# Samples' attention: a 512-column product of a constant ahead of each group of four transposes

## The reference, cut to what matters

```python
D_MODEL, HEAD_DIM, KV_HEADS, HEADS_PER_GROUP = 1024, 64, 2, 4     # 8 heads
# q: (8 samples, 1, 2, 4, 64); ks_blk, vs_blk: 2048 past rows + the new one, in blocks of 64
_, idx = lax.top_k(score, min(N_SEL_BLOCKS, nsel))     # score: from the compressed branch
k_sel, v_sel = ks_blk[bi, gi, idx], vs_blk[bi, gi, idx]
s_s = jnp.einsum('bqghd,bgqkld->bghqkl', q, k_sel) * scale + b_s
o_s = jnp.einsum('bghqm,bgqmd->bqghd', masked_softmax(s_s, tpos <= qp), v_sel)
s_w = jnp.einsum('bqghd,bkgd->bghqk', q, kw) * scale + rel_bias_heads(rel_bias, dw)
o_w = jnp.einsum('bghqk,bkgd->bqghd', masked_softmax(s_w, window_mask), vw)
o = g[..., 0:1] * o_c + g[..., 1:2] * o_s + g[..., 2:3] * o_w
```

## Time and profile before

| | |
|---|---|
| median of 3 runs | 2104.97 us |
| lowest, highest | 2093.45, 2114.90 us |
| profiled execution: time | 2103.55 us |
| its span | 2101.7 us |
| TensorE (PE) busy in the span | 1978.6 us, 94% |
| PE weight loads | 1899.4 us, 90% |
| VectorE (DVE), ScalarE (ACT), GpSimd (POOL) busy | 830.1, 647.1, 795.4 us |
| mean granted TensorE clock | 0.961 |

### The profile page before, as it was taken

One profiled execution on the slowest core, in us unless ns is written; L12 is line 12 of the kernel. 1 busy time (PEld: TensorE's weight loads), 2 busy tenths in 40 slices (PEclk: granted clock), 3 DMA queues, 4 the chain that ended last, 5 costly groups with the idle time before them and its releaser, 6 DMA issues. The chain is left out here.

```text
span 2101.7 us, 35304 instructions
## 1 busy us (share of the span) xinstructions
PE 1978.6 (94%) x14462; PEld 1899.4 (90%) x14462; DVE 830.1 (39%) x1560; ACT 647.1 (31%) x1159; POOL 795.4 (38%) x639
## 2 busy tenths in 40 slices
PE   7999989966799998999989899999999999999899
PEld 6999989944678888999989899999999999999699
DVE  4013534323677875112241359333333430322633
ACT  5112035422577674001011223223332310200333
POOL 2223300000345454333333215777777733332140
PEclk9999989977899999999999889999999999999999
DMA  7233374343400002111113121222332232321212
GB/s 245 62 91 121 81 244 161 121 162 129 149 2 2 1 2 82 46 46 46 46 36 131 41 108 49 76 90 81 120 101 80 80 121 74 119 79 51 81 41 81
DMA packets 168156, 182.62 MB, mean 87 GB/s; under 512 B 21176, under 2 KB 151810, under 8 KB 165154
## 3 DMA queue, kind: packets, MB, share of 16 engines
q1 hardware_dynamic: 162034, 131.48, 20.1%
q0 software_dynamic: 2304, 33.56, 4.1%
q10 hardware_dynamic: 3696, 15.86, 2.0%
HBM read 148.12 MB, written 36.94 MB: 88 GB/s over the span
## 5 line engine op out<-in xcount | busy, mean ns | idle before, releaser
L603 POOL CAST WS<-W 128x1024 fp32r<-128x1024 f32 (+1 forms) x87 | 96.3, 1106 | 551.2 <-PE proj_acc L595 147.6
L2480 PE MATMUL ffn_acc<-ZR,WR 128*128 128x258 f32 x1976 | 293.9, 283 | 0.6 <-POOL WR L2405 0.6
L2480 PEld LDWEIGHTS ffn_acc<-ZR,WR 128*128 128x128 f32 x1976 | 262.0, 190 | 0.8 <-POOL WR L2405 0.8
L605 POOL TENSOR_TENSOR WS<-W,WS 128x1024 fp32r<-128x1024 f32 (+1 forms) x87 | 215.0, 2471 | 7.0
L2405 POOL TENSOR_TENSOR WR<-WQ,WR 128x512 fp32r<-128x512 f32 x114 | 172.0, 1515 | 101.4 <-ACT WR L2618 101.4
L2480 PE MATMUL ffn_acc<-HH,WR 128*128 128x258 f32 x1216 | 202.3, 283 | 3.5 <-issue 2.2
L2733 DVE TENSOR_TENSOR E<-E,ffn_acc 128x516 f32<-128x516 f32 x133 | 92.0, 692 | 237.6 <-PE ffn_acc L2480 234.8
L595 PE MATMUL proj_acc<-HH,WS 128*128 128x344 f32 x912 | 174.3, 324 | 7.6 <-DVE HL L527 7.6
L2480 PEld LDWEIGHTS ffn_acc<-HH,WR 128*128 128x128 f32 x1216 | 170.1, 190 | 4.0 <-issue 2.5
L595 PEld LDWEIGHTS proj_acc<-HH,WS 128*128 128x128 f32 x912 | 149.0, 189 | 8.4 <-issue 6.1
L595 PE MATMUL merge_acc<-HH,WS 128*128 128x344 f32 x768 | 146.9, 324 | 6.8 <-DVE HL L527 6.8
(11 more groups left out here) (480 smaller groups left out, 4152.5 us busy)
## 6 DMA issues: line engine op xcount, KB each, us to landing
W<-in_w_in SPq DMA_DIRECT2D x30, 512.0 KB, 3.9
gated_values<-E ACTq DMA_DIRECT2D x22, 516.0 KB
WQ<-in_w_ffn_up SPq DMA_DIRECT2D x38, 256.0 KB, 2.9
WQ<-in_w_ffn_gate SPq DMA_DIRECT2D x38, 256.0 KB, 3.1
W<-in_w_ffn_down SPq DMA_DIRECT2D x16, 384.0 KB, 3.1
W<-in_w_ffn_down SPq DMA_DIRECT2D x16, 320.0 KB, 3.0
kept_x<-Z SPq DMA_DIRECT2D x1, 4128.0 KB, 13.3
Z<-kept_x SPq DMA_DIRECT2D x1, 4128.0 KB, 13.4
```

What stands on the lines that cost most here:

```text
L603: k.nc.gpsimd.tensor_copy(k.WS[:, ws, 0, 0:nk, :], w).then_inc(hi_done, 1)
L605: k.nc.gpsimd.tensor_tensor(k.WS[:, ws, 1, 0:nk, :], w, k.WS[:, ws, 0, 0:nk, :].bitcast(F32), ALU.subtract).then_inc(split_done, 1)
L2480: last = nc.tensor.matmul(acc[:, b + h, 0:QN], k.WR[:, RING[j], part, c, :], src[:, c, h * QN:(h + 1) * QN], start=(c == 0 and part == 0 a ...
```

## The change

Each group of four transposes, in `keys` and in `turn_p`, gets one product ahead of it: 128x128 weights and 512 columns, both taken from `QZ` as float32r, written to the whole bank that the four transposes overwrite. It stands behind the wait for the bank. There are 50: 40 in `keys`, 10 in `turn_p`. `QZ` is filled once, at the head of VectorE's list, with eight copies of the 128x128 identity, and TensorE waits for that (`dense_in`) ahead of its first product of the stage.

```diff
+        (dense_in,) = st.sems("dense_in")
+        dense = k.QZ[:].rearrange("p a b c m -> p (a b c m)")
...
                 bank = tp_bank(pe, ("keys", i, q, j))
+                nc.tensor.matmul(bank, dense[:, 0:P], dense[:, 512:1024], start=True, stop=True)
                 for x in range(4):
...
                 bank = tp_bank(pe, ("p", i, x, 0))
+                nc.tensor.matmul(bank, dense[:, 0:P], dense[:, 512:1024], start=True, stop=True)
                 src = (PA, PA, PB, PB, PW)[x][:, (0, 512, 0, 512, 0)[x]:]
...
+            pe.wait_ge(dense_in, 1)
             pe.wait_ge(k.sel_in, 7 * 16)
             pe.wait_ge(qs_placed, 4)
...
         def _(dve):
+            nc.vector.tensor_copy(dense.rearrange("p (r m) -> p r m", r=8), k.ident[:].unsqueeze(1).to_broadcast([P, 8, P])).then_inc(dense_in, 1)
             nc.vector.memset(QS, 0.0).then_inc(qs_placed, 1)
```

## The result

The changed kernel takes 2116.09 us (median of 20 runs, 2106.64 to 2123.33) against 2102.82 us for the kernel before, measured beside it (20 runs). The ratio is 1.0061, with a 95% interval of 1.005 to 1.0072: 13 us slower, within the 1% that was called "same", inside the range of 2098 to 2121, and 6 us above the number 2109.9. The profiled execution of the changed kernel has a span of 2119.4 us, before 2101.7: 17.7 us more. It took 2121.24 us and so is 5 us above the median of its kernel.

A forecast was written before the change was run, and what follows sets the result against it. PE's own work, partly at half clock, was taken to bound the samples' attention. Cast 1.1 plus products 13.5 less 1.0 absorbed is 13.6 us; less 7.25 for A held, 6.35 us slower: 2109.9 us, range 2098 to 2121.

The forecast's parts named there:

- A is held: Samples' attention, 447.2 to 460.9 us: the added products keep the clock at 1.00 there, giving back 7.25 us.
- A: Samples' attention from 447.2 us: 13.7 us at 0.50 of the clock, forecast to run at 1.00.
- Rival 1: Samples' attention: the clock stays where it was and the products only cost; 13.6 us slower, 2117.2 us; chance 0.33.
- B: Samples' attention from 474.5 us: 3.4 us at 0.50 of the clock, forecast to stay so.
- Between them it is at 1.00: Samples' attention: the clock was read as 1.00 between the four stretches at 0.50.
- C: Samples' attention from 502.7 us: 9.4 us at 0.50 of the clock, forecast to stay so.
- Cast, 1.1 us: Head of VectorE's list: the cast that fills QZ delays PE's first product of the stage by 1.1 us, nothing hiding it.
- Products, 0.23 and 0.43 us: Groups of transposes: each added product costs 0.23 us at clock 1.00 and 0.43 at 0.50; 44 on the path, 13.5 us.
- Rival 1's sum, 13.6 us: Samples' attention without any clock change: 1.1 for the cast, 13.5 for products, less 1.0 absorbed by bank copies.
- the clock in the stages behind moving: Stages after the samples' attention: example given for "something else", the case outside forecast and rivals; chance 0.03.
- The six hidden products: Half 1's groups of samples 4, 5 and 6: six products, 2.6 us, fit under PE's waits of 7.99 and 4.17 us.

The follow-up runs named there:

- keys-only kernel: The kernel before plus the cast and the forty products ahead of the keys' groups, none ahead of P's turns: 2111.23 us, ratio 1.0035.
- the change with the fill: The changed kernel plus twelve unread products in the feed-forward stage where PE waits for the rounded rows: 2107.58 us, ratio 1.004 to the kernel before.
- the kernel with the feed-forward fill alone: The kernel before plus twelve unread products in the feed-forward stage where PE waits for the rounded rows: 2100.96 us, ratio 1.0006.

## Why the prediction was right or wrong

The range held and the chances of "same" too, but only since the range was wide enough for the rival. The number was 6 us low, and the failed step is **"A is held"**. I gave back 7.25 us for it; the trace gives back nothing there. The argument for it compared the share of full-array products (0.23 in each 0.67 us of a group) with that of `scores` between 460.9 and 474.5, and took an equal share as enough. That was a likeness and no evidence: it compared a stretch that already had 1.00 with one that had to get there. The runs show in its place that the clock in A stays at 0.50 with one product per group. Three kernels with one product per group have A at 0.50 for 13.7 us or more, two kernels with two products have 3.4. Rival 1's chance of 0.33 was too small beside the 0.45 of the forecast. But rival 1 isn't the mechanism either. It said that the clock is where it was, and B, which the forecast left at 0.50, was at 1.00 in all five kernels with products ahead of the turns.

**A reading of the earlier trace rows.** "Between them it is at 1.00" is not so between B and C: the clock was at 0.50 from 491.6 on, mostly while PE waited for the gathers. The sum doesn't change by it, since the two groups in that time lie under a wait.

**Cast, 1.1 us.** It took 0.69, below even the lower bound of 0.91 for clearing the buffer. With the 0.07 us to the next start and the 0.24 by which the copy of `relb` is longer it cost 1.0, so the term was nearly right by a part that wasn't in it.

**Products, 0.23 and 0.43 us.** 0.38 at 0.50. At 1.00 a set of four groups grew by 0.79 us where 0.67 was worked out from the banks' rhythm: the copies absorb 0.13 of four products, not 0.25.

**Rival 1's sum, 13.6 us, to the stage.** The total came out at 13.3, but not as summed. To the end of half 0 the profile has +8.3 us where "about 8" stood, with A 6.8 us longer than before, which wasn't predicted. In the keys-only kernel and in the change with the fill, A was 13.7 us, and the time from the stage's first product to the gather was 49.5 and 49.1 us against 44.8 before: +4.7 and +4.3, not 7. Behind it, 19 products less the absorption should have added about 5.5 us more (8 x 0.43 + 11 x 0.23 - 0.5 for the copies), and +0.17 came; in the pair with the fill it is +3.9 (62.0 against 58.1). In the changed kernel's profile C ended 6.4 us sooner against sample 7's keys, worth up to 3.2, and sample 6's keys came 10.92 us after their gather's start and not 12.21, worth 1.3 (gathers at 492.64 and 484.37). Whether the product did the first is open, and the other runs speak against it: with the same products C ended 8.1 and 8.5 us after sample 7's keys (keys only; change with the fill), and 7.9 us in the kernel with the feed-forward fill alone, which has none. Nor is the second clearly the product's: sample 6's keys came 10.8 to 12.7 us after the gather in twelve profiles, 10.91 in the one with the cast only.

**The stage as a whole.** From its first product to the prompt's attention it is 110.7 and 111.1 us in the two profiles that hold the change, and 101.7 to 105.7 in six that hold nothing of it but, in one, the cast. So some 7 us is the change's, against 13.6 minus the cast predicted. With the cast that is about the 8.3 and 8.8 us of S x c in the two pairs, though these count another thing. The spread of the six has a part that can be seen: where the clock was at 1.00 for 3.4 us just ahead of A, half 0 took 44.8 us, and where that was missing, 47.1.

**The stages behind: 0.03 for "the clock in the stages behind moving".** That was the second miss, though it does not change the verdict. In the profile 9.6 us arise there. In the medians it is some 5 us, if the stage took 8 of the 13; that is argued. I had summed the stage to its last wait and taken the rest as a constant, while the page's slices 23 and 24 of the earlier trace rows show another dip to 0.8 that a shift of 8 us can lengthen or shorten.

**The gathers and waits.** 4.61 and 3.24 us are left of 7.99 and 4.17. The six hidden products fit under them, as said.

## What to carry to other kernels

Ballast for the clock, that is products whose result nothing reads, pays where PE waits anyway: 38 products in two DMA waits gave a kernel faster by 0.16%, while 50 among the groups gave one slower by 0.61%, and twice as many held the clock but cost the 20 us that this gave back. Don't take a result that is near the forecast for the mechanism: read the clock of the stretch that the forecast names. Read how a stage's length varies between profiles of identical code before a few microseconds in it are explained. And when a shift is put into a stage, look for slow stretches in all the stages behind it, since those change with the moment of entry.

## What the runs showed that I had not expected

The head of the feed-forward stage is at 0.50 for 17.1 to 47.8 us, over profiles with the same instructions there, but for the hold in three of them. Holding its start by 1.2, 2.4 and 3.6 us moved the kernel's time by -2.7, +4.9 and -4.7 us. The same instructions in the samples' attention, but for the cast in one, took 101.7 to 105.7 us. One product per group took away the 3.4 us at 0.50 in half 0's turns and left A. And products in place of idle time did no harm that is seen to the DMAs that landed meanwhile: the keys of sample 7 came 18.5 us after the gather with the 38 products and 18.4 in the kernel before, and the other profiles have 17.0 to 18.8.
